# Twenty of the 24 conditioning blocks move into the convolution's norm and the attention, and the 32 sample rows are multiplied in four strips

## The reference, cut to what matters

```python
def ada_mod(c, w, b):                       # w is 1024 x 6144 in each layer
    return jnp.split(jax.nn.silu(c) @ w + b, 6, axis=-1)
def modulate(x, g, shift, scale):
    return rmsnorm(x, g) * (1 + scale[:, None, :]) + shift[:, None, :]
...
# layer 0: attention and a 31-tap convolution share one input and one output projection
proj = h @ w_in                             # 1024 x 2560
q, k, v, ga, gb = jnp.split(proj, [...], axis=-1)
...                                         # differential attention; the samples also read the paged cache
u = ga * jax.nn.sigmoid(gb)
cv, new_buf = causal_dwconv(u, conv_buf, cb_w)
cv = jax.nn.silu(layernorm(cv + cb_b, cb_ln_g, cb_ln_b))
out = jnp.concatenate([o, cv], axis=-1) @ w_out          # 1024 x 1024
# layer 1: bg, cg, hx = split(h @ w_in, 3)  (1024 x 3072); out = (bg * conv3(cg * hx)) @ w_out
# each layer: x += gate1 * out; h = modulate(x, g2, shift2, scale2); x += gate2 * moe(h)
# moe: 4 groups x 8 experts, top group, then its top 2 experts
```

## Time and profile before

| | |
|---|---|
| median of 3 runs | 2338.16 us (2332.77 to 2342.81) |
| the profiled execution's own time | 2338.08 us |
| its span in the profile | 2336.3 us |
| PE busy | 1805.1 us, 77% of the span |
| DVE busy | 489.2 us, 21% |
| ACT busy | 320.0 us, 14% |
| bytes moved | 604.27 MB, mean 259 GB/s |

### The profile page before, as it was taken

The page is one execution under the profiler, slowest core; times in us unless marked ns, Lnnn a source line. Parts: engine busy times, 40 slices in busy tenths (PEclk is TensorE's granted clock), DMA queues, the critical chain, the costliest instruction groups (busy, mean ns, idle before and its releaser), DMA issues. The chain is left out here.

```text
span 2336.3 us, 26113 instructions
## 1 busy us (share of the span) xinstructions
PE 1805.1 (77%) x8631; PEld 848.3 (36%) x8632; DVE 489.2 (21%) x1006; ACT 320.0 (14%) x590; POOL 148.8 (6%) x157
## 2 busy tenths in 40 slices
PE   4779994558796778888887639998957888787782
PEld 1345432234444233333332225555343333332231
DVE  0016783442124011001000041111140000000003
ACT  1120213332201000101010030000110101000001
POOL 0000121001111000000000030000110000000004
PEclk8769997569896799999999969999958999999896
DMA  9991207427703778999999950200167989999994
GB/s 355 387 381 22 73 35 276 196 61 258 269 0 122 298 286 313 389 384 410 393 411 411 404 186 0 72 1 2 54 254 272 408 331 411 409 411 411 411 410 169
DMA packets 194116, 604.27 MB, mean 259 GB/s; under 512 B 15952, under 2 KB 18289, under 8 KB 193898
## 3 DMA queue, kind: packets, MB, share of 16 engines
q1 hardware_dynamic: 162800, 522.55, 57.7%
q10 hardware_dynamic: 21025, 46.17, 5.3%
q0 software_dynamic: 10208, 34.48, 4.1%
HBM read 551.57 MB, written 52.01 MB: 258 GB/s over the span
## 5 line engine op out<-in xcount | busy, mean ns | idle before, releaser
L811 PE MATMUL ps<-ring,W 128*64 128x512 f32 x2048 | 473.5, 613 | 52.5 <-issue 28.0
L824 PE MATMUL ps<-ring,W 128*64 128x512 f32 x1024 | 281.5, 699 | 51.2 <-DVE W L1660 48.0
L811 PEld LDWEIGHTS ps<-ring,W 128*64 128x64 f32 x2048 | 175.3, 141 | 339.1 <-issue 338.8
L940 ACT ACTIVATE W<-ps 128x512 f32<-128x512 f32 (+3 forms) x241 | 133.5, 567 | 949.7 <-PE ps L824 372.4
L1654 DVE TENSOR_TENSOR W<-W,ps 128x256 f32<-128x256 f32 x64 | 26.9, 421 | 807.5 <-ACT W L1221 807.5
L918 PE MATMUL ps<-hT,ring 128*128 128x512 f32 x384 | 170.7, 597 | 0.5 <-DVE W L1680 0.5
L824 PEld LDWEIGHTS ps<-ring,W 128*64 128x64 f32 x1024 | 93.1, 159 | 198.8 <-issue 198.8
L563 PE MATMUL ps<-ring,hT 128*128 128x512 f32 (+1 forms) x240 | 108.2, 607 | 1.9 <-DVE W L1360 1.9
L918 PEld LDWEIGHTS ps<-hT,ring 128*128 128x128 f32 x384 | 71.1, 190 | 80.9 <-issue 80.4
L481 PE MATMUL ps<-ring,cT 128*32 128x512 f32 x384 | 70.3, 871 | 23.3 <-DMA ring<-in_w_ada_dram 23.1
L1345 DVE SCALAR_TENSOR_TENSOR W<-W,prm 128x512 f32<-128x512 f32 x116 | 85.3, 804 | 0.0
(11 more groups left out here) (286 smaller groups left out, 1489.4 us busy)
## 6 DMA issues: line engine op xcount, KB each, us to landing
ring<-in_w_gate_up_dram SPq DMA_DIRECT2D x128, 2048.0 KB, 16.4
ring<-in_w_down_dram SPq DMA_DIRECT2D x64, 2048.0 KB, 16.7
ring<-in_w_ada_dram SPq DMA_DIRECT2D x24, 2048.0 KB, 19.8
x_rows<-X ACTq DMA_DIRECT2D x1, 18944.0 KB, 50.6
ring<-in_cache_k_dram SPq DMA_DIRECT2D x64, 256.0 KB, 3.0
W<-x_rows SPq DMA_DIRECT2D x32, 512.0 KB, 17.5
x_rows<-W ACTq DMA_DIRECT2D x128, 128.0 KB, 5.9
ring<-in_cache_v_dram POOLq DMA_DIRECT2D x48, 256.0 KB, 4.6
```

What stands on the lines that cost most here:

```text
L811: x = mm(ps[CAP * z:CAP * z + CAP, 2 + j, :], xt[:, k, :], at[:, :, 256 * z:256 * z + 256], start=(k == 0), stop=(k == KD - 1))
L824: x = mm(ps[CAP * z:CAP * z + CAP, 5 + j, :], ht[:, k % 2, CAP * (k // 2):CAP * (k // 2) + CAP], ring[:, 3 * j + 2, at:at + 512], start=(k ...
L940: return fn(out, src, ACT.Copy, **k)
```

## The change

It does two things. First, only conditioning blocks 0 to 3 (shift and scale of layer 0's first norm) are multiplied before meet 0. They land in slots 2 to 5, and the five blocks of `w_in` follow them at once. Block 4 goes to slot 5, blocks 5 to 7 to slots 2 to 4 as Q, K and V free them, and each later block to the slot of the block four earlier. Products 4 to 6 stand in the convolution's norm, products 7 to 22 in the 16 steps of the attention, product 23 behind them. Each keeps its ACT copy, its four turns and its DVE add; bank 7 holds both product and turns, so the heads' outputs all use bank 6. The loops become straight code. The first value pages are issued behind meet 3, both `w_out` blocks behind the conditioning blocks, the loads of `X` ahead of the parameters, and the copy over `x_rows` at the end of meet 0.

Second, the 32 sample rows of every projection are multiplied as the conditioning rows are: eight products with the samples as the 32 stationary columns, in four strips (`sample_strips`), one ACT copy (`sample_row`), and then for token-major results one 32x512 product that sums the strips (`strip_sum`), for channel-major results one 128x32 product for each 128 channels (`strip_turn`).

```diff
@@ sync
+            for n in range(ADA0):
+                ada_load(n)
             for s, col in enumerate((3, 4, 0, 1, 2)):
-                sp.wait_ge(slot_free[s], 5)
+                if s >= 2:
+                    sp.wait_ge(S["ada_mm"], s - 1)
                 load(s, wina[:, :, 512 * col:512 * col + 512])
+            sp.wait_ge(S["ada_mm"], ADA0)
+            ada_load(ADA0)
...
-            sp.wait_ge(S["tok_mm"], 3 * NT)
+            for n in range(ADA0 + 1, ADA):
+                if n < ADA0 + 4:
+                    sp.wait_ge(S["tok_mm"], NT * (n - ADA0))
+                else:
+                    sp.wait_ge(S["ada_mm"], n - 3)
+                ada_load(n)
@@ tensor
+            def sample_strips(b, src, s):
+                for k in range(KD):
+                    z = 32 * (k % 4)
+                    x = mm(ps[z:z + 32, b, :], src[:, k, TP:T], tile8(s)[:, k, :], start=(k < 4), stop=(k >= 4),
+                           skip_group_check=True)
+                x.then_inc(S["smp_mm"], 1)
+            def strip_turn(to, rowbuf, m):
+                return mm(to, rowbuf[:, P * m:P * m + P], C[:, C_SUM:C_SUM + NS], start=True, stop=True)
+            def strip_sum(n, to, rowbuf):
+                pe.wait_ge(S["smp_ok"], n + 1)
+                return mm(to, C[:, C_SUM:C_SUM + NS], rowbuf, start=True, stop=True)
...
@@ attention steps, tensor
                     scores(u + 1)
+                pe.wait_ge(S["ada_ev"], u + 7)
+                ada_product(u + 7, 7)
                 pe.wait_ge(S["at_p"], u + 1)
...
                 x.then_inc(S["at_tr"], 1)
+                row_turns(u + 7, 7, W_AR)
@@ attention steps, scalar
                     exps(u + 1)
+                ada_row(u + 7, 7, W_AR)
                 act.wait_ge(S["at_tr"], u + 1)
@@ attention steps, vector
                 stt(out=e0, in0=e0, scalar=st[:, at:at + 1], in1=e1, op0=ALU.mult, op1=ALU.add).then_inc(S["at_p"], 1)
+                ada_mod(u + 7, 7)
                 if u % 4 == 2 and u > 4:
                     norm_scale(u // 4 - 1)
```

More of the change, by code:

```diff
@@ L470, in _ @@
[L470 to L485, removed]
@@ L486, in _ @@
-            meet(pe, 0)
+            for n in range(ADA0):
+                if n >= 2:
+                    pe.wait_ge(S["row_ok"], n - 1)
+                ada_product(n, n % 2)
+                if n == 0:
+                    pe.wait_ge(S["params_in"], 16 * 9)
+                    tr(ps[:, 6, 0:96], W[0:96, 0:P], ident[0:96, 0:96])
+                    tr(ps[:, 6, 96:165], W[0:69, P:2 * P], ident[0:69, 0:69])
+                    tr(ps[:, 6, 165:289], W[0:124, 2 * P:3 * P], ident[0:124, 0:124]).then_inc(S["prm_tr"], 1)
+                    continue
+                if n >= 3:
+                    pe.wait_ge(S["ada_ev"], n - 2)
+                row_turns(n - 1, 2 + (n - 1) % 2, W_ROW + 512 * ((n - 1) % 2))
@@ L558, in _ @@
                 if i == 0:
-                    pe.wait_ge(slot_in[s], 80)
+                    pe.wait_ge(slot_in[s], 32)
+                if i == LS - 1:
+                    sample_strips(5, hT, s)
                 if u >= 4:
                     pe.wait_ge(S["tok_copy"], u - 3)
-                for k in range(KD):
-                    x = mm(ps[0:rows(i), u % 4, :], hT[:, k, toks(i)], tile8(s)[:, k, :],
-                           start=(k == 0), stop=(k == KD - 1))
+                if i == LS:
+                    x = strip_sum(SMP_QKV + u // NT, ps[0:NS, u % 4, :], sg[:, 0:512] if u < 2 * NT else raw[:, 2, :])
+                else:
+                    for k in range(KD):
+                        x = mm(ps[:, u % 4, :], hT[:, k, toks(i)], tile8(s)[:, k, :], start=(k == 0), stop=(k == KD - 1))
                 x.then_inc(S["tok_mm"], 1)
@@ L593, in _ @@
                 x.then_inc(S["ln_mm"], 1)
+                if c == 1:
+                    row_turns(4, 7, W_AR)
+            for n in (5, 6):
+                pe.wait_ge(S["ada_ev"], n)
+                ada_product(n, 7)
+                row_turns(n, 7, W_AR)
             meet(pe, 2)
@@ L1003, in norm @@
                 rms(l, 1)
+                if l == 0:
+                    for n in range(2, ADA0):
+                        act.wait_ge(S["row_tr"], n - 1)
+                        ada_row(n, n % 2, W_ROW + 512 * (n % 2))
                 layer_wait(act, l, "rms1_inv", 1)
@@ L1012, in norm_ev, with sample_row @@
                        bias=mod(l, 0)[:, c, 0:1]).then_inc(L["ev1a"], 1)
+            def sample_row(n, b, to):
+                act.wait_ge(S["smp_mm"], n + 1)
+                copy(to, ps[:, b, :]).then_inc(S["smp_ok"], 1)
             def gates(l, name, to=w(W_G, D), to_s=w(W_GS, D, rows=NS), b=4):
@@ L1180, in ffn @@
             def ffn(l, k0):
+                for n in range(2):
+                    sample_row(SMP_WO[l] + n, 4 + n, smp_rows_wo[n])
                 for i in range(NT):
@@ L1246, in _ @@
             for c in range(KD):
+                if c % 4 == 0:
+                    for s in range(3):
+                        sample_row(SMP_IN + 3 * (c // 4) + s, 3, smp_rows[s])
                 act.wait_ge(S["bch_mm"], c + 1)
@@ L1393, in _ @@
                 tt(cv[:, c, :], cv[:, c, :], sg, ALU.mult).then_inc(S["ln_n"], 1)
+            for n in (5, 6):
+                ada_mod(n, 7)
             meet(dve, 2)
@@ L1738, in cache @@
                     pool.dma_start(ring[:, 2 + n % 2, 512 * k:512 * k + 512], cvp[page, :, :]).then_inc(v_in[n % 2], 16)
+            meet(pool, 2)
+            meet(pool, 3)
             pool.wait_ge(S["page_in"], 16)
@@ L1742, in _ @@
             cache(1)
-            meet(pool, 2)
-            meet(pool, 3)
             for n in range(2, 6):
```

211 lines of the change are left out of this document (129 added, 82 removed).

## The result

The changed kernel takes **2182.7 us** (median of 4 runs, 2176.7 to 2189.9) beside 2336.4 us (4 runs, 2332.8 to 2342.8) for the kernel before on the same chip: ratio 0.934, 95% interval 0.930 to 0.938. In a later set of five runs it took 2185.2 us, ratio 0.9365 (0.9342 to 0.9389). It was forecast at 2213 us, 2188 to 2243. So the gain is 154 us by the first measurement and 147 by the second, where 125 were forecast. The sign and the front were right, and the attention was charged too much: 20.6 us of the 30 between 2213 and 2182.7 are its. Another 7.2 are the distance of the profiled execution, 2189.85 us, from the median, and 2.6 are all other terms together.

A forecast was written before the change was run, and what follows sets the result against it. Modulation was taken as DMA-bound, most projections PE-bound, Q and K DVE-paced, prompt attention an engine chain. Terms -115 - 8 - 4 + 3 + 32 + 3 + 2 - 14 - 24 = -125 from 2338 gave 2213 us, range 2188 to 2243.

The forecast's parts named there:

- The sign: Whole kernel: faster by over 0.5% (12 us), chance 0.97; slower 0.02, no change 0.01.
- the front: Start to convolution input: only four conditioning blocks needed, so that input starts at 51 us, not 166; gain 115.
- the attention: Prompt attention: conditioning added in 16 steps costs +32 us at a mixed clock, and +3 behind the last step.
- the convolution input: Convolution input projection: eight groups of short records leave, two strips and eight turns come; net -8 us.
- Q, K and V: Q, K and V projections: strips save 4 us for V; Q and K gain nothing because DVE sets the pace.
- the convolution's norm: Convolution's norm: three conditioning products, with their copies, turns and adds, cost +3 us (bounds +1 and +6).
- The full-clock price: Prompt attention at full clock: product hides, turns cost 1.06 plus about 0.4, scores give back about 0.7 a step; +12 us.
- I take 0.70: Prompt attention: clock assumed 0.70, four tenths of the time at full speed, so 45 - 0.4 x 33 = +32 us.
- The first rival: Prompt attention: the fuller PE holds the clock high, so +12 in place of +32 us, total 2193; chance 0.20.
- The half-clock price of +45: Prompt attention at half clock: product overflows PE's wait and turns lie bare, 2.5 to 3.5 us, 16 times; +45.
- The strips: Sample rows as strips: each output projection -7 us, layer 1's input projection -24; a tiling switch under 0.1 us.
- The sample attention: Sample attention: value pages and `w_out` blocks, 8 MB, now move at its start; +2 us (0 to 16).

The follow-up runs named there:

- the first pair: The first profiles of the kernel before and of the changed kernel, compared phase by phase; span -148.2 us.
- the second pair: Both kernels, unedited, profiled a second time in the last set of runs and compared phase by phase; span -163.2 us.
- experiment 7: Two 128x512 products added to each of the 16 attention steps of the kernel before; 2328.5 us beside 2332.1, ratio 0.998 (0.996 to 1.001).

## Why the prediction was right or wrong

*The front and the convolution input* (-123): right, -123.9 and -124.7. The first turn of the norm came at 43.05 us (forecast "about 44"), and the input's first strip at 50.77, forecast 51. Loads ran at 351 GB/s, less than the 375 used, and it made no difference that can be seen.

*Q, K and V* (-4) and *the convolution's norm* (+3): right, within about 2 us. Q and K are still paced by VectorE: behind each of their sample tiles PE now waits 4.8 and 4.9 us for POOL, where the longest such wait was 0.7. The copy over `x_rows`, which I had as a possible 5 to 15 us, cost nothing: PE has no wait for the Q block.

*The attention* (+32, and +3 behind it): **this is the step that failed.** It measured +14.4 and +15.0. The full-clock price was sound: it was +12, and by the variants it is 127.1 - 114.4 = +12.7 against the same kernel without conditioning, made of 23.5 us of turns and copies less the 10.8 by which the products shortened the phase. What failed is the sentence "I take 0.70", and with it the weighing of two prices by the mean clock of the phase. I read the clock off two windows of the modulation (0.79 and 0.63), where the same products and turns run without the softmax between them, and off a PE busy time that I had worked out at half clock, so that the estimate began from the state that it was to decide. The first rival, "the clock rises in the attention", had the right price and the right time for the phase (125 us at a clock above 0.85; it was 127 at 0.84). It had a chance of 0.20, and it should have been the forecast: in the old attention PE was busy half the time, and the wait in each step was the very place where a product now stood. The Trainium skill, page "TensorE: Matmul & The Clock Gate", section "The HAM clock gate", has activity as what releases the throttle. The prediction set this rule behind the two windows; the runs side with the rule here, since each version with products has the higher clock (0.84 to 0.93 against 0.56 to 0.61). Not every added work did it, though: copies, turns and adds alone left the clock at 0.56.

The clock alone is not the whole miss. At the measured 0.84 the forecast's own rule, 45 - 0.68 x 33, would still have given +23 and not +12. In the trace of the changed kernel the low clock mostly missed the priced instructions: 11 of the 16 products took 1.92 us and 13 of the 16 groups of turns 1.06, while the values at the end of a head took 4.4 to 4.6 us in three heads, beside 2.40 in the first. So the mean clock of a phase is not the clock of what is added to it. The half-clock price of +45 was never measured, since no version with products stood at the low clock.

With the +14.4 of the first pair in place of +35 the sum is 2192.5, the rival's time, 2.6 us above the execution that was profiled. What is left in that pair is +8.8 in the sample attention, -8.3 in the experts of layer 1, and small terms.

*The strips* (output projections -7 each, layer 1's input projection -24): right for layer 1, and the number right by luck for layer 0. The output projection of layer 1 gave 7.8 and 7.9. That of layer 0 gave 8.7 in one pair and 4.4 in the other. What the prediction had at +1, the last prompt tile's chain being less covered, is PE's wait for DVE ahead of the norm's products, and it grew by 5.2 us, in both pairs; first before, then now:

```profile
710.86 1.97 PE L789 MATMUL ps<-C,Hb 128*128 128x128 f32 x16 [0.77 <-DVE W L1539]
```
```profile
611.60 3.29 PE L856 MATMUL ps<-C,Hb 128*128 128x128 f32 x16 [5.97 <-DVE W L1648]
```

The first pair hides this loss, because the small products behind it stood at half clock before and at full clock in the changed kernel (3.47 and 1.87 us for sixteen records); in the second pair they stood at full clock in both. The input projection, from its first strip to the turns behind it, takes 190 us where it took 214, -24.0. The strips showed no price for changing the shape. The Trainium skill, page "TensorEngine Tiling (Array Packing)", section "Key Properties", has a drain at each switch of mode; nothing of the 10 us that it could have cost here is to be seen in these phases.

*The sample attention* (+2): the mechanism is there and the size is about right, but the first pair of profiles hides it. From the keys to the second weights the kernel before took 96.9 and 97.1 us, and the changed one 99.7 and 99.4, with a key wait of 9.1 to 9.4 in place of 4.3 to 4.7: +2.5. The other +8 of the first pair is the tail at 50.9 against 42.9 us; in the second pair it is 42.7 against 54.5. My bound "over 145 us would be wrong" was therefore a bad test, since the kernel before itself goes past it, at 151.6.

*The experts* (0): -8.3 and -0.5 in layer 1, with eleven profiles of kernels that share this code between 601.8 and 618.5. This is scatter, as is the median's distance from the first profile: that execution, 2189.85 us, was the slowest of its four. The low end of my range had no room for it. 2188 was the high-clock case less a part of its own width, reckoned against one execution.

## What to carry to other kernels

Where a phase is a chain with TensorE half busy at a low granted clock, independent TensorE work put into its waits can cost less than nothing: price it at both clocks, and do not weigh the two prices by a mean clock read elsewhere. A gain in the phase has still to be shown in the whole time: of the 11 us of experiment 7 it was not. Put such work where the chain waits (behind the scores), and keep its short dependent parts (the turns) out of the place ahead of the instruction that the other engines need next; that order alone was worth 11 us in the attention here at the same clock, and 19 where the clock was higher too. And profile the kernel before twice ahead of reading a phase difference: two phases of the same kernel differed by 12 and 7 us between executions.

## What the runs showed of the hardware that was not expected

- Work added to TensorE made a phase shorter: 111.5 to 100.4 us in the kernel before, 114.4 to 103.6 and 144.6 to 127.1 in the changed one.
- The busy share alone did not tell the clock here. With turns alone PE was busy 85.2 of 144.6 us at clock 0.56; with products alone it was busy 74.5 of 103.6 at 0.87; in the modulation before, 23.3 of 27 at 0.63.
- Behind one wait of 3.83 us the executions of one kernel part: the same work takes 42.9 or 54.5 us in the kernel before, as TensorE's clock is back after the first strip or not at all, and 42.7 or 50.9 in the changed one, where it was back after the first strip or the third. Four products in the wait (0.29 us of it left) brought the weights behind it from 3.67 to 2.00 us, both times.
